# Sparse-branch prompt scores as three products of rounded high and low parts, in a two-layer hybrid encoder

## The reference, cut to what matters

```python
a_q = rope(heads(a_q), pos)
a_k = rope(a_k, pos)
...
s = jnp.einsum('bqhd,bkd->bhqk', q.astype(f32), kg) * HEAD_DIM ** -0.5
s = jnp.where(valid[:, None], s, NEG)
p = jax.nn.softmax(s, axis=-1)
return jnp.einsum('bhqk,bkd->bqhd', p, vg).astype(q.dtype)
```

## Time and profile before

| | us |
|---|---|
| median of 3 runs (range) | 2135.39 (2135.14 to 2136.21) |
| the profiled execution | 2135.8 |
| its span | 2133.9 |
| TensorE busy, matmuls | 2113.4 |
| VectorE busy | 1338.5 |
| ScalarE busy | 991.7 |
| GpSimd busy | 191.5 |

### The profile page before, as it was taken

The page is one execution under the profiler, slowest core; times in us unless marked ns, Lnnn a source line. Parts: engine busy times, 40 slices in busy tenths (PEclk is TensorE's granted clock), DMA queues, the critical chain, the costliest instruction groups (busy, mean ns, idle before and its releaser), DMA issues.

```text
span 2133.9 us, 40042 instructions
## 1 busy us (share of the span) xinstructions
PE 2113.4 (99%) x16142; PEld 2002.3 (94%) x16142; DVE 1338.5 (63%) x2537; ACT 991.7 (46%) x1611; POOL 191.5 (9%) x138
## 2 busy tenths in 40 slices
PE   7999999999999999999999999999999999999998
PEld 7898998898999999999998989889989999999998
DVE  6668736776556773576465686377766377636753
ACT  5357414646525652344342672155465276424431
POOL 0000000000031110011300100000000401100112
PEclk9999999999999999999999999999999999999999
DMA  5231223121122222222232213221211222232222
GB/s 196 71 110 38 82 76 113 41 80 51 50 80 83 85 89 90 89 79 89 90 116 80 85 40 100 80 95 51 72 48 61 82 87 79 89 91 87 81 87 95
DMA packets 53492, 175.06 MB, mean 82 GB/s; under 512 B 6704, under 2 KB 11392, under 8 KB 53360
## 3 DMA queue, kind: packets, MB, share of 16 engines
q1 hardware_dynamic: 46896, 158.88, 24.1%
q0 software_dynamic: 2688, 9.95, 1.2%
q10 hardware_dynamic: 3776, 4.34, 0.6%
HBM read 160.25 MB, written 12.90 MB: 81 GB/s over the span
## 4 chain that ended last, share of the span: by engine, by line
PE 96%; DVE 2%; ACT 1%; DMA 0%; issue 0%; ACTq 0%; SPq 0%; DVEq 0%
PE d L1373 61%; PE d L1423 14%; PE ab L1469 4%; PE d L1434 2%; PE ab L1701 2%; PE d L1753 2%; PE d L1744 2%; PE d L1614 1%; PE d L1473 1%; PE ab L1694 1%; PE ab L1731 1%; PE ab L1373 0%; PE ab L1520 0%; PE d L1867 0%; PE ab L1551 0%; PE d L1568 0%
## 5 line engine op out<-in xcount | busy, mean ns | idle before, releaser
L455 ACT ACTIVATE wh<-raw 128x512 fp32r<-128x512 f32 x548 | 345.0, 631 | 722.6 <-PE d L1373 585.4
L799 DVE TENSOR_TENSOR wl<-raw,wh 128x512 fp32r<-128x512 f32 x548 | 378.4, 692 | 314.7 <-ACT wh L455 305.6
L1373 PE MATMUL d<-xh,wh 128*128 128x288 f32 x2400 | 514.6, 295 | 8.6 <-DVE wl L797 8.6
L1373 PE MATMUL d<-xl,wh 128*128 128x288 f32 x2400 | 511.9, 294 | 0.0
L1373 PE MATMUL d<-xh,wl 128*128 128x288 f32 x2400 | 511.7, 294 | 0.0
L1373 PEld LDWEIGHTS d<-xh,wh 128*128 128x128 f32 x2400 | 384.1, 189 | 12.1 <-issue 10.7
L1373 PEld LDWEIGHTS d<-xl,wh 128*128 128x128 f32 x2400 | 383.9, 189 | 0.0
L1373 PEld LDWEIGHTS d<-xh,wl 128*128 128x128 f32 x2400 | 383.7, 188 | 0.0
L1423 PE MATMUL d<-xh,wh 128*128 128x288 f32 x768 | 173.3, 307 | 0.5 <-DVE g L905 0.5
L1423 PE MATMUL d<-xh,wl 128*128 128x288 f32 x768 | 164.5, 295 | 0.0
L1423 PE MATMUL d<-xl,wh 128*128 128x288 f32 x768 | 164.3, 295 | 0.0
(11 more groups left out here) (319 smaller groups left out, 3276.7 us busy)
## 6 DMA issues: line engine op xcount, KB each, us to landing
raw<-in_w SPq DMA_DIRECT2D x288, 512.0 KB, 3.5
out_o_k<-k POOLq DMA_DIRECT2D x4, 1152.0 KB, 7.1
out_o_v<-v POOLq DMA_DIRECT2D x4, 1024.0 KB, 8.7
x<-in_xT SPq DMA_DIRECT2D x8, 288.0 KB, 6.1
out_y<-z SPq DMA_DIRECT2D x16, 144.0 KB, 1.9
k<-in_bc_k_past ACTq DMA_DIRECT2D x4, 512.0 KB, 5.0
v<-in_bc_v_past ACTq DMA_DIRECT2D x4, 512.0 KB, 6.9
w<-in_masks SPq DMA_DIRECT2D x1, 800.0 KB, 5.1
```

The costliest lines, as they stand in the source:

```text
L455: act.activation(wh[:, c % SPLIT_SLOTS, :], stored, ACT.Copy).then_inc(high_done, 1)
L799: dve.tensor_tensor(lows, stored, highs, ALU.subtract).then_inc(low_done, 1)
L1373: ins = pe.matmul(outs[half], w_, r_[:, kk, HALF * half:HALF * half + HALF], start=first and n == 0 and begin, stop=last and n == len(kks) ...
```

## The change

The f32 product of each prompt score tile in branch A becomes three products of fp32r operands: high query x high key, low query x high key, high query x low key. kh (high) and kl (low) are the first 512 columns of the keys, made once a layer; qh and ql are those of the pair's queries, made once a pair. ScalarE makes the high parts by a copy, VectorE the low parts by a subtraction. kl and ql lie in the place of their sources k2 and q; kh and qh in a place where past keys of the other branches were. The stream tokens' scores, and branches B and C, stay as they are.

The key parts are made at j = 0 of the queries. The high part of query 0 is made at j = 2 on ScalarE, behind the wait for query 2 and ahead of the shift; its low part on VectorE behind the rope of query 1. For pair p + 1, the high part stands behind `exp_step(3)` of pair p, the low part behind `scale_step(3)`. TensorE's wait for the rope of query p in `scores_wide` becomes a wait for the low parts.

```diff
+            def key_high(l):
+                act.wait_ge(st_k, 16 * (2 * l + C + 1))
+                act.wait_ge(chosen_ready, l + 1)
+                act.activation(kh[:], k2[:, 0, 0:TP], ACT.Copy).then_inc(k_highs, 1)
+
+            def query_high(l, p):
+                act.wait_ge(roped, l * 8 + 5 + p)
+                act.activation(qh[:], q[:, p, 0:TP], ACT.Copy).then_inc(q_highs, 1)
...
                             wait_taken(act, l, D_Q[m] + j)
                             if j == 0:
-                                act.wait_ge(chosen_ready, l + 1)
+                                key_high(l)
                             if j == 2:
-                                act.wait_ge(roped, l * 8 + 5)
+                                query_high(l, 0)
                             shift(q[:, j, :], scores[:, T * (j % 2):T * (j % 2) + T])
...
                         exp_step(3)
+                        if m == A and p < PAIRS - 1:
+                            query_high(l, p + 1)
                         turn_step(2)
...
+            def query_low(l, p):
+
+                dve.wait_ge(q_highs, l * PAIRS + p + 1)
+                dve.tensor_tensor(ql[:, p, 0:TP], q[:, p, 0:TP], qh[:].bitcast(F32), ALU.subtract).then_inc(q_lows, 1)
...
                         take_query(l, m, j)
+                        if m == A and j == 0:
+                            dve.wait_ge(k_highs, l + 1)
+                            dve.tensor_tensor(kl[:], k2[:, 0, 0:TP], kh[:].bitcast(F32), ALU.subtract).then_inc(k_lows, 1)
...
                         if m == A and j:
                             rope(l, 2 + j, q[:, j - 1, :], scores[:, T * ((j - 1) % 2):T * ((j - 1) % 2) + T])
                         if m == A and j == 2:
+                            query_low(l, 0)
                             max_step(l, m, 0, 0)
...
                         scale_step(l, m, p, 3)
+                        if m == A and p < PAIRS - 1:
+                            query_low(l, p + 1)
                         low_parts(l, cg + 5)
...
+                                if m == A:
+                                    for i, r in enumerate(ROWS):
+                                        pe.matmul(ab[:, bank + i, a:a + n], qh[r, tile], kh[r, 0:n], start=a == 0, stop=False, skip_group_check=True)
+                                    for i, r in enumerate(ROWS):
+                                        pe.matmul(ab[:, bank + i, a:a + n], ql[r, p, tile], kh[r, 0:n], start=False, stop=False, skip_group_check=True)
+                                    for i, r in enumerate(ROWS):
+                                        pe.matmul(ab[:, bank + i, a:a + n], qh[r, tile], kl[r, 0:n], start=False, stop=False, skip_group_check=True)
+                                    continue
...
                             if m == A:
 
-                                pe.wait_ge(roped, l * 8 + 5 + p)
+                                pe.wait_ge(k_lows, l + 1)
+                                pe.wait_ge(q_lows, l * PAIRS + p + 1)
                             score_tiles(p, ((3, 0, 0),))
```

More of the change, by code:

```diff
@@ L158, in encoder @@
         xl = sb("xl", [P, KD, T], F32R)
-        q, k, v, g, _, oh, _, ol, ah, al = shared(
+        q, k, v, g, _, oh, kh, qh, ol, ah, al, ql = shared(
             [("q", [P, 4, T], F32), ("k", [P, 4, KEYS], F32), ("v", [P, 7, HEADS * HD], F32),
              ("g", [P, KD, T], F32)],
-            [("over_q", [P, 4 * T], F32), ("oh", [P, 4, T], F32R), ("rest_of_k", [P, 4 * PAST], F32),
+            [("over_q", [P, 4 * T], F32), ("oh", [P, 4, T], F32R), ("kh", [P, 512], F32R), ("qh", [P, 512], F32R),
              ("ol", [P, 4, T], F32R)],
-            [("ah", [P, FH, T], F32R), ("al", [P, FH, T], F32R)])
-        k2, _, chosen = shared(
+            [("ah", [P, FH, T], F32R), ("al", [P, FH, T], F32R)],
+            [("ql", [P, 4, T], F32R)])
+        k2, kl, _, chosen = shared(
             [("k2", [P, 2, KEYS], F32)],
+            [("kl", [P, TP], F32R)],
             [("over_k2", [P, KEYS], F32), ("chosen", [P, 1664], BF16)])
@@ L238, in encoder @@
         roped = sem("roped")
+        k_highs, k_lows, q_highs, q_lows = sem("k_highs"), sem("k_lows"), sem("q_highs"), sem("q_lows")
         past_i, past_b, past_c = sem("past_i"), sem("past_b"), sem("past_c")
@@ L1698, in score_tiles @@
                             for t, bank, a in places:
-                                n = tile_keys(t)
+                                n, tile = tile_keys(t), slice(t * P, (t + 1) * P)
+                                if m == A:
[6 more added lines that the diff above has]
+                                    continue
                                 for i, r in enumerate(ROWS):
-                                    pe.matmul(ab[:, bank + i, a:a + n], q[r, p, t * P:(t + 1) * P], keys(r, p)[:, 0:n], start=a == 0, stop=False, skip_group_check=True)
+                                    pe.matmul(ab[:, bank + i, a:a + n], q[r, p, tile], keys(r, p)[:, 0:n], start=a == 0, stop=False, skip_group_check=True)
                             for t, bank, a in places:
```

## The result

| | before | after |
|---|---|---|
| median of 6 runs (range), us | 2135.12 (2134.77 to 2136.21) | 2146.38 (2144.45 to 2149.27) |
| ratio to before, 95% interval | | 1.0054 (1.0043 to 1.0064) |
| profiled execution, span, us | 2135.8, 2133.9 | 2147.35, 2145.6 |

A forecast was written before the change was run, and what follows sets the result against it. TensorE, busy for 99% of the span, was taken to bound the kernel. Tiles -1.24, first wait +4.27, clock +2.7 and pair 0 to 1 -0.5 made +5.2 us a layer, +10.5 in both: 2145.9 us, range 2139.5 to 2150.

The forecast's parts named there:

- The tiles: Score tiles on TensorE: three rounded products save 0.31 us a pair, -2.5 us for four pairs in two layers.
- both rivals on that: Score tiles: loads not hidden between one head's products, 2152 us, chance 0.06; heads run in turn, 2160 us, chance 0.05.
- The first wait: Ahead of pair 0's scores: TensorE waits for query 0's low part, queued behind query 1's rope, +4.27 us a layer.
- the rival on the other side: Ahead of pair 0's scores: query 0's parts come early, the wait is covered, no clock lost; 2133 us, chance 0.04.
- The clock: Behind the first wait: TensorE's granted clock halves after the idle stretch, +2.7 us a layer, bounds nothing and 3.4.
- Pair 0 to 1: From pair 0's to pair 1's scores: VectorE and ScalarE ahead after the stall, -0.5 us a layer, bounds -0.8 and +0.2.
- nobody ahead: Pair 1's scores: the +0.2 us bound, query 1's low part at 504.2 plus hand-over, with VectorE and ScalarE not ahead.
- For pairs 1 and 2: Ahead of pair 2's scores: the low part ends at 526.2, TensorE comes at 527.42, hidden with 1.2 us to spare.
- Nothing: Key parts at query 0: copy and subtraction (0.63 + 0.68 us) fall where both engines have microseconds free, costing nothing.
- The sum: Whole kernel: -1.24 + 4.27 + 2.7 - 0.5 = +5.2 us a layer, +10.5 us for both, giving 2145.9 us.

The follow-up runs named there:

- e9: e1 with the score products of the kernel before (f32), the low parts written to scratch and not read: 2136.04 us, ratio 1.0002.
- e1: The changed kernel with query 0's high part moved ahead on ScalarE and its low part to the head of j = 2 on VectorE: 2133.84 us, ratio 0.9994.
- e2: The changed kernel with 30 useless products on TensorE ahead of each layer's first wait for the low parts: 2141.92 us, ratio 1.0033.
- e3: The changed kernel with f32 score products, all copies, subtractions and waits kept, low parts to scratch: 2148.66 us, ratio 1.0064.
- e7: e2 with 15 useless products instead of 30: 2145.03 us, ratio 1.0048.
- e5: e1 with pair 0's second maximum and second exponential ahead of the tenth chunk's low and high parts: 2134.81 us, ratio 0.9996.
- e8: The kernel before, with only pair 0's second maximum and exponential moved ahead of the tenth chunk's parts: 2136.79 us, ratio 1.0006.
- e4: e3 with TensorE waiting for the rope alone, so nobody waits for the copies and subtractions: 2137.23 us, ratio 1.0008.
- e6: e5 with the next query's high part behind the third exponential and its low part ahead of the fourth maximum: 2136.25 us, ratio 1.0003.

## Why the prediction was right

*The tiles* (-1.24 a layer, -2.5 in all). Measured in place 0.27 a pair against 0.31 forecast: 0.17, 0.02 and 0.08 for the terms 0.19, 0.03 and 0.09. As a whole: e9 against e1 2.2 us by the medians and 1.0 a layer inside the traces, less than four times 0.27 or 0.31, since pair 0 gives nothing. The heads run side by side and the loads are hidden behind 512, 384 and 256 columns; both rivals on that fall. So does, for these products, the rule of the Trainium skill (TensorE: Matmul & The Clock Gate, Part 3, what overlaps and what doesn't) that a weight load overlaps a running product only in another row group. The second and third 512 product share their row groups and stand 0.23 apart, where load and columns in series would need 0.32.

*The first wait* (+4.27 a layer). 4.27 in both layers, by the same steps: taking, rope of query 1, low part. e1 shows that the order of the queues makes it, as the rival on the other side had it: with the parts made early the kernel takes 2133.84 (forecast for that case 2133).

*The clock* (+2.7 a layer). In the profiled execution 5.6 and 6.8 us at 1.2 GHz, 2.8 and 3.4 us lost there, 2.5 and 3.0 of it reaching the way to pair 1's scores. By the medians of after and e2 it is 4.5 us for both layers, 2.3 each. That 2.7 came so near was in part luck: it was priced from one fall. In the trace of e3 the clock cost 1.6 us in layer 0, and in e7 3.0 in one layer and nothing in the other. In the six runs of after the time follows the clock; span and mean granted clock of each:

```
2142.7 0.997   2143.3 0.997   2143.6 0.996   2145.6 0.995   2146.3 0.994   2147.5 0.993
```

Not all of it is the new wait's doing: the eleven runs of e1, which has no such wait, scatter by 4.0 us, with clocks of 0.999 (2130.4) to 0.997 (2134.4).

*Pair 0 to 1* (-0.5 a layer). This step failed: it had a gain of 0.5 us, and nothing was gained. I reasoned that after the stall VectorE and ScalarE are ahead by 0.6 us, and that the waits in pair 0 shrink. The chain is not anchored at the stall: ScalarE's tenth high part waits for TensorE's first half of the fourth projection, and the second maximum and the second exponential stand behind it. The trace of before had shown it already, with a shorter wait. ScalarE's timelines of before and after, and the first transposes of both:

```profile
486.13 0.63 ACT L455 ACTIVATE wh<-raw 128x512 fp32r<-128x512 f32 x1 [0.36 <-PE d L1373]
492.27 1.04 PE L1744 MATMUL d<-cf,w 128*128 128x128 f32 x8
```
```profile
491.56 0.63 ACT L458 ACTIVATE wh<-raw 128x512 fp32r<-128x512 f32 x1 [3.51 <-PE d L1398]
497.70 1.03 PE L1778 MATMUL d<-cf,w 128*128 128x128 f32 x8
```

From this copy to the first transposes it is 6.14 us (491.56 to 497.70), in before too (486.13 to 492.27), and from the transposes to the gate product that waits 7.36 us in both. So nothing is regained, the 256 tile's 0.08 is swallowed besides, and the low part of query 1 costs what was worked out for "nobody ahead", some +0.2. It ends at 509.56 (508.87 + 0.69) and the scores start at 509.71, where the last transposes (509.01) with the 0.48 of before would put them at 509.49.

```profile
508.87 0.69 DVE L913 TENSOR_TENSOR ql<-q,qh 128x512 fp32r<-128x512 f32 x1
```

That my first idea for removing the rest of pair 0's wait (e5, e8) made it longer shows that I hadn't read this chain fully. It has two sides, the fourth projection and ScalarE's own queue, and moving one instruction past the other trades them. How much of pair 0's wait an order could remove stays open; none that I tried did.

For pairs 1 and 2 the parts were to be hidden, and are: the way from pair 1's scores to pair 2's is 23.03 and 23.05 in after against 23.36 and 23.29, shorter by about the tiles' 0.27. "Nothing" for the key parts was not tested by itself.

*The sum.* By the medians the loss is 11.3 us, 5.6 a layer. Of that -1.1 is the tiles (e9 against e1) and +2.3 the clock (after against e2). This leaves 4.5 for the first wait with the small loss in pair 0 (4.27 and some 0.2 to 0.3). The forecast's 5.2 was 0.4 a layer too low in total: 0.7 to 0.8 too good for pair 0, 0.1 too good for the tiles, 0.4 too high for the clock. The mechanism was right, but that the whole came out within 0.5 us is luck: these errors cancel in part, and the runs of after alone scatter by 4.8 us.

## What to carry to other kernels

Here the instructions that make a new operand cost little in themselves (e9 against the kernel before: 0.7 us by the medians, 0.4 for both layers inside the traces); what it costs is decided by what stands ahead of them in the in-order queues of the engines that make it. Before adding a wait on the bounding engine, list for each step behind which instruction it is queued, and ask whether that instruction itself waits for the bounding engine's latest work: here this made +11.3 us out of products that save 2.2, and two moved calls took it back. Where a wait on TensorE can't be avoided, add the lost clock to it, here half of the wait again.

## What the runs showed of the hardware that I had not expected

- The clock fell also 0.6 and 0.8 us after the work had resumed (layer 1 of after, layer 0 of e7), not only inside the idle stretch. In both layers of after and in layer 0 of e7 it was low for 6.8 us (481.4 to 488.3, 1543.0 to 1549.8, 483.5 to 490.3), in layer 0 of e3 for 3.4 us only. What it costs is how much of that lies over work: 2.5 us where it fell inside the wait and 3.0 where it fell later, both in after.
- The wait of the earlier trace rows, from which the prediction priced the clock, stands in every trace (2.5 to 3.1 us). The clock was low behind it for 6.8 us in before, e4 and e9, for 3.4 us in after, e1, e2, e3, e6, e7 and e8, and not at all in e5, where the wait was 2.72 us. One trace can't give the price of such a wait.
- 2.30 us of idle time were enough once and not the other time in one and the same execution (e7). What decides it can't be told from these runs.
- Useless products in a wait made the kernel 4.5 us faster (e2).
- Products of 64 rows and 128 columns stand 0.11 us apart, the pace of their loads, though by the 0.213 us for 512 their columns need half of that. The 128 and 384 tiles together gained 0.02 us from the rounded format, the 512 tile 0.17: its gain lies in wide tiles.
